# One elementwise step of a mixture-of-experts loop moves from VectorE to GpSimd

## What is computed

```python
gu = lax.ragged_dot(xs, w_gu, group_sizes) + b_gu[e_sorted]     # xs: tokens sorted by expert, 1024 wide; gu: 2048 wide
gate, up = jnp.split(gu, 2, axis=-1)
gate = jnp.minimum(gate, 7.0)
up = jnp.clip(up, -7.0, 7.0)
act = (up + 1.0) * gate * jax.nn.sigmoid(1.702 * gate)
out = lax.ragged_dot(act, w_down, group_sizes) + b_down[e_sorted]
```

## Time and profile before

| what | value |
|---|---|
| median of 3 runs | 5977.84 us (5977.51 to 5979.96) |
| the profiled execution, its own time | 5979.14 us |
| its span | 5977.5 us |
| PE busy | 5781.5 us, 97% of the span |
| DVE busy | 4260.5 us, 71% |
| ACT busy | 3097.3 us, 52% |
| POOL busy | 919.0 us, 15% |
| low parts of gate and up weights on DVE (L2185) | 648 times, 2283 ns each |
| low parts of down weights on DVE (L2191) | 324 times, 2284 ns each |

### The profile page before, as it was taken

The page is one execution under the profiler, slowest core; times in us unless marked ns, Lnnn a source line. Parts: engine busy times, 40 slices in busy tenths (PEclk is TensorE's granted clock), DMA queues, the critical chain, the costliest instruction groups (busy, mean ns, idle before and its releaser), DMA issues. The chain is left out here.

```text
span 5977.5 us, 78741 instructions
## 1 busy us (share of the span) xinstructions
PE 5781.5 (97%) x27604; PEld 4693.8 (79%) x27604; DVE 4260.5 (71%) x3445; ACT 3097.3 (52%) x2879; POOL 919.0 (15%) x694
## 2 busy tenths in 40 slices
PE   7999999999999989999879999999999999999996
PEld 3788888887777768887758888888888888888883
DVE  4333322005665665556889999999999999999996
ACT  5222100114444444442157777777777777777771
POOL 1000000003333320000001111111111111111113
PEclk9999999999999999999989999999999999999998
DMA  6322111213444455555357533317367459532355
GB/s 236 133 74 74 60 53 53 74 72 118 138 135 136 134 170 183 184 184 183 113 197 306 214 123 120 123 32 267 129 239 290 143 211 413 191 95 60 130 207 189
DMA packets 307087, 924.08 MB, mean 155 GB/s; under 512 B 26721, under 2 KB 164193, under 8 KB 272161
## 3 DMA queue, kind: packets, MB, share of 16 engines
q1 hardware_dynamic: 215664, 701.07, 31.9%
q0 software_dynamic: 40496, 169.27, 10.0%
q10 hardware_dynamic: 50784, 51.92, 2.5%
HBM read 744.01 MB, written 178.27 MB: 154 GB/s over the span
## 5 line engine op out<-in xcount | busy, mean ns | idle before, releaser
L2185 DVE TENSOR_TENSOR moe_w_lo<-keep_w_gu,moe_w_hi 128x2048 fp32r<-128x2048 f32 x648 | 1440.3, 2283 | 2.3 <-ACT moe_w_hi L2131 2.3
L2131 ACT CAST moe_w_hi<-keep_w_gu 128x2048 fp32r<-128x2048 f32 x648 | 1238.6, 1912 | 376.8 <-PE moe_ps_gu L2074 190.2
L2191 DVE TENSOR_TENSOR moe_w_lo<-moe_w_dn,moe_w_hi 128x2048 fp32r<-128x2048 f32 x324 | 733.5, 2284 | 31.9 <-ACT moe_w_hi L2141 31.9
L2141 ACT CAST moe_w_hi<-moe_w_dn 128x2048 fp32r<-128x2048 f32 x324 | 620.4, 1915 | 256.1 <-PE moe_ps_gu L2074 256.1
L2074 PE MATMUL moe_ps_gu<-moe_w_hi,moe_hT_hi 128*128 128x512 f32 x2592 | 702.6, 393 | 12.3 <-DVE moe_w_lo L2185 12.3
L2074 PE MATMUL moe_ps_gu<-moe_w_lo,moe_hT_hi 128*128 128x512 f32 x2592 | 694.0, 390 | 0.0
L2074 PE MATMUL moe_ps_gu<-moe_w_hi,moe_hT_lo 128*128 128x512 f32 x2592 | 693.5, 389 | 0.0
L168 PE MATMUL prj_ps_p<-h_hi,prj_w_hi 128*128 128x512 f32 x1760 | 685.9, 390 | 7.2 <-DVE prj_out L795 6.5
L168 PE MATMUL prj_ps_p<-h_lo,prj_w_hi 128*128 128x512 f32 x1760 | 685.4, 389 | 0.0
L168 PE MATMUL prj_ps_p<-h_hi,prj_w_lo 128*128 128x512 f32 x1760 | 685.4, 389 | 0.0
L2074 PEld LDWEIGHTS moe_ps_gu<-moe_w_lo,moe_hT_hi 128*128 128x128 f32 x2592 | 487.5, 188 | 101.9
(11 more groups left out here) (340 smaller groups left out, 9434.5 us busy)
## 6 DMA issues: line engine op xcount, KB each, us to landing
keep_w_gu<-in_w_gu_t SPq DMA_DIRECT2D x128, 2048.0 KB, 11.6
moe_w_dn<-in_w_down_t SPq DMA_DIRECT2D x64, 2048.0 KB, 8.9
rows_scratch<-prj_out POOLq DMA_DIRECT2D x47, 1024.0 KB, 4.4
across_w<-in_w_in_t SPq DMA_DIRECT2D x80, 512.0 KB, 4.4
moe_b_gu<-b_gu_scratch SPq DMA_DIRECT2D x32, 1024.0 KB, 8.1
nin_w<-in_w_ada SPq DMA_DIRECT2D x48, 512.0 KB, 6.0
rows_scratch<-across_late ACTq DMA_DIRECT2D x96, 256.0 KB, 2.8
ssd_xT<-rows_scratch SPq DMA_DIRECT2D x64, 256.0 KB, 3.2
```

The lines of the kernel that those rows point to most:

```text
L2131: act.copy(w_hi[n % NB][:], raw(w_gu, n)).then_inc(gu_hi, 1)
L2141: act.copy(w_hi[(GU + n) % NB][:], raw(w_dn, n)).then_inc(dn_hi, 1)
L2185: dve.tensor_tensor(w_lo[n % NB][:], raw(w_gu, n), w_hi[n % NB][:].bitcast(F32), ALU.subtract).then_inc(gu_lo, 1)
L2191: dve.tensor_tensor(w_lo[b][:], raw(w_dn, n), w_hi[b][:].bitcast(F32), ALU.subtract).then_inc(dn_lo, 1)
```

## The change

The cut of `up` between its two limits is no longer a DVE instruction between the last low part of the down weights and the product with `gate`. POOL makes it, in place, from SBUF. POOL's instruction waits for `up` to have been added (`u_added`), and it stands in POOL's step behind the store and the fetch. DVE's product at L2206 waits, as before, on the semaphore `u_cut`, which now comes from POOL.

```diff
@@ POOL's part of experts() @@
+                def cut_up(i):
+                    pool.wait_ge(u_added, i + 1)
+                    apart(pool, S)
+                    pool.tensor_scalar(up[:], up[:], LIMIT + 1.0, 1.0 - LIMIT, ALU.min, ALU.max).then_inc(u_cut, 1)
+
                 def step(at):
                     at(4, store)
                     at(0, fetch_tokens)
+                    at(2, cut_up)
@@ DVE's part of experts() @@
                 def gate_up(i):
-                    dve.wait_ge(u_added, i + 1)
-                    dve.tensor_scalar(up[:], up[:], LIMIT + 1.0, 1.0 - LIMIT, ALU.min, ALU.max).then_inc(u_cut, 1)
                     dve.wait_ge(u_cut, i + 1)
                     dve.wait_ge(g_added, i + 1)
                     dve.scalar_tensor_tensor(out=up[:], in0=gate[:], scalar=LIMIT, in1=up[:], op0=ALU.min, op1=ALU.mult).then_inc(gated, 1)
```

## The result

| | before | after |
|---|---|---|
| median | 5977.68 us (11 runs) | 5993.24 us (11 runs, 5989.62 to 5997.09) |
| ratio of the runs | | 1.0026, 95% interval 1.0017 to 1.0035 |
| profiled execution | 5979.14 us | 5994.53 us, span 5992.9 us |

The forecast was 75 us more; it is 15.6 us more. The direction was as predicted, and so was the place of half the loss; one term of the sum, the time that the cut itself takes, was far too large. First the durations of the instructions that write or read `up` in the changed kernel (ns min/median/max, first and last start).

A forecast was written before the change was run, and what follows sets the result against it. PE, busy throughout the steady expert stage, was taken as the bound. 0.93 us of idle PE in 79 steps, 73.5 us, plus 1.1 and 0.5 for first and last tile, made 75 us: 6053 us, range 5993 to 6110.

The forecast's parts named there:

- PE bounds, removing DVE work gains nothing: Steady expert stage: PE is busy 2720.00 of 2720.00 us, so removing another engine's work cannot shorten it.
- The ring and its small slack: Each expert step: PE, ACT, DVE's chain and PE's first unit form a closed ring with about 0.05 us slack.
- a wait elsewhere: Sign against the prediction: PE showing waits elsewhere than at the first gate and up unit of each step.
- DVE's wait at the third down unit: In each step DVE's 0.39 us wait moves along with PE and stays, at about 0.35.
- PE's clock: Expert stage: PE's clock shouldn't suffer from the waits; after 2.04 us of waiting a matmul shows the full-speed 0.39 us.
- When the cut can run, and shut out by the low part: POOL's cut stands still until DVE's fourth low part ends at 4529.55, keeping only 0.14 us of start-up as overlap.
- the cover holds: Rival, chance 0.10: the cut runs unblocked beside the fourth low part and ends before it; time stays at 5978.
- How long the cut takes, 1.70 us: POOL's cut of 1024 columns was put at 1.70 us, from L331's 2.79 us less DVE's 1.09 us of possession.
- the cut is cheap: Rival, chance 0.15: the cut costs the memset's 0.951 us, 0.18 us a step beyond the slack: 15 us, 5993.
- the cut is dear: Rival, chance 0.18: the cut takes 2.36 us, giving 6105, or L331's whole 2.79, giving 6140.
- The first tile, 1.1 us: First tile: no low part beside the cut; POOL's 1.70 us replace 0.69 where PE waits anyway, costing 1.1 us.

The follow-up runs named there:

- turned_after: Changed kernel with DVE making hT_lo between the bias additions and the fourth low part, beside POOL's cut: 5976.17 us, ratio 0.9996 to the kernel before.
- cut_one_op: Changed kernel with POOL applying only the upper limit, the cut's lower limit left out: 6132.66 us, ratio 1.0260.
- cut_neutral: Changed kernel with POOL applying the same minimum twice and no lower limit: 6227.89 us, ratio 1.0419.
- one_input: Changed kernel with DVE's fourth low part reading PSUM in place of w_hi, so one SBUF input: 5977.48 us, ratio 1.0000 to the kernel before.

## Why the prediction was right and wrong

- **PE bounds, removing DVE work gains nothing:** right. turned_after takes the cut off DVE at no cost, and its ratio of 0.9996 can't be told from 1.
- **The ring and its small slack:** the ring is right, its tight spot is not. The prediction let PE lose everything at the first unit of the next step, and called a wait elsewhere a sign against itself. PE waits at the third unit as well. From the third unit's weight load to the next step's first it is 29.09 us (4544.12 - 4515.03) where it was 28.98 (4534.91 - 4505.93): 0.11 more. From the first unit's load to the third's it is 5.54 (4549.66 - 4544.12) where it was 5.44 (4540.35 - 4534.91): 0.10 more. Those 5.54 us are what DVE takes from the end of the first low part to the end of the third (4544.06 to 4549.60), with the product L2215 between them. So the slack that counts is the third unit's. It was put at 0.05 us and is about 0.1 by the table above. The 0.05 was 0.17 less the 0.11 of the earlier trace rows; in the steady state a waiting load starts only 0.06 us behind the low part (4544.06 to 4544.12). And a load that is a little late doesn't hold up its matmuls yet: undisturbed they start 0.23 us behind it, after a wait 0.03 us (4544.12 and 4544.15).
- **DVE's wait at the third down unit** doesn't simply move along with PE: it shrank from 0.39 to 0.28 us. The prediction had about 0.35.
- **PE's clock:** right for this change, 1.00 in the stage. It was still 1.00 with 1.53 us of idle PE in a step (cut_one_op); with 2.39 us (cut_neutral) it fell in every fourth.
- **When the cut can run, and shut out by the low part:** right. It ended 0.91 us after the low part did, its undisturbed 1.04 less the 0.14 us of start-up that the prediction read off. The same subtraction gives 2.64 us for cut_one_op, measured 2.63 (4540.34 less 4537.71), and 3.50 us for cut_neutral, measured 3.49 (4549.80 less 4546.31). The rival "the cover holds" falls with it. The Trainium skill, page "SBUF — State Buffer", section "Who interferes with whom", has the rule of the two SBUF inputs; one_input against the changed kernel bears it out, 1037 against 2901 ns.
- **How long the cut takes, 1.70 us:** wrong, and it is the step that failed. It was taken from L331 by splitting its 2.79 us between two engines that were thought to exclude each other. L331 isn't of the cut's kind. A single addition costs 2.78 us beside an idle DVE, on 32 partitions as on 128, so L331 had lost nothing to DVE. The cut as min+max costs 1.04. With 1.04 in the prediction's own sum, the product is 0.32 us late (4529.55 + 0.90 + 0.06 = 4530.51), 0.27 beyond the slack of 0.05, and 79 steps give 21 us. With the slack that the runs show it is 17. Of the 59 us between forecast and result this price makes 52 (0.66 us in 79 steps) and the slack 4.
- **The rival "the cut is cheap"** was the right one; it gave 5993 and got 0.15. It leaned on a memset, 0.951 us, and the cut came within 0.09 of it. That it hit 5993 to the microsecond is luck: its price was 0.09 us too low and its slack 0.05 too small, and the two errors nearly cancel. The Trainium skill's "roughly line-rate" for one input ("GPSIMD Engine Reference", section 4.1) fits this pair of operations, and doesn't fit the single operations (2.78 us) or the other pairs (3.64 us).
- **The rival "the cut is dear"** with L331 whole, 6140 us, is what a cut with one operation would have cost: 6133.
- **The first tile, 1.1 us:** the product starts 2.95 us after the addition of `up` (3079.35 to 3082.30) where it was 1.97 (3081.01 to 3082.98), 1.0 more. The cut is undisturbed there, 1037 ns. POOL's own fetch DMA (3080.19 to 3081.16) held it until 3081.22, and the product started at 3082.30, after 1.73 us in which DVE was idle. The size was about right, the reason incomplete.

## What to carry to other kernels

The elementwise step given to GpSimd cost nothing beside a DVE instruction with one SBUF input, and 16 us beside one with two; look for such a neighbour in DVE's order before moving work. Take a GpSimd price from the very pair of operations in the very order: a neighbour in kind was off by 2.7 times here, and swapping two limits cost 4%. And where an engine is 99% busy in a ring with one that is 100% busy, count the slack at each unit that the late engine feeds, not at the first alone, and not the idle time that the profile shows somewhere else.

## What the hardware showed that was not expected

- GpSimd's TENSOR_SCALAR on 1024 fp32 columns: min+max, add+mult, mult+add, mult+mult took 1.04 to 1.05 us; a single min, max, add or mult 2.77 to 2.79; max+min, min+min, add+max, add+add, min+mult, mult+min 3.64 to 3.65. The 512-column rows, 0.61 and 1.50 us, show that the difference is per column. Why is open.
- A blocked GpSimd read can be passed over more than once. In one_input, POOL's copy of a single column took 12014 ns in the median. POOL's timeline and DVE's, in one step:

```profile
5295.84 12.02 POOL L2047 COPY moe_home_i<-keep_slot_home 128x1 int32 x1 [10.01 <-ACT moe_rows L2162]
```

```profile
5298.92 8.89 DVE L2191 TENSOR_TENSOR moe_w_lo<-keep_w_gu,moe_w_hi 128x2048 fp32r<-128x2048 f32 x4
5307.73 1.22 DVE L2224 TENSOR_TENSOR moe_aT_lo<-moe_ps_t,moe_aT_hi 128x1024 fp32r<-128x1024 f32 x1
```

  It ended at 5307.86, just after DVE had gone over to an instruction that reads PSUM, having been passed by at each boundary between two low parts. In the neighbouring step at 5330.27 the same copy took 1.00 us. The cut isn't open to this, as DVE's next instruction waits for it and leaves DVE idle; no run shows a long instruction without such a wait.
- The one instance in which GpSimd came first shows no exclusion for a whole instruction; it was not tried separately. L331, first by 0.13 us, took 2.79 us, as beside an idle DVE, while DVE's L466 beside it was held up for 0.75 us and finished 0.68 us before L331 did.
